# The first recurrence's triangular inverse in 32x32 blocks on four array tiles

## What is computed

```python
def step(S, inp):
    r_t, w_t, k_t, v_t, a_t, b_t = inp
    sa = jnp.einsum("bhvk,bhk->bhv", S, a_t)
    S = S * w_t[:, :, None, :] + sa[..., None] * b_t[:, :, None, :] + v_t[..., None] * k_t[:, :, None, :]
    y = jnp.einsum("bhvk,bhk->bhv", S, r_t)
    return S, y
```

## Time and profile before

| what | value |
|---|---|
| median of the timed runs | 2913.34 us |
| lowest and highest | 2909.52, 2915.71 us |
| span of the profiled execution, first to last instruction | 2905.3 us |
| mean granted TensorE clock in it | 0.995 |
| TensorE busy, of that span | 2814.7 us (97%) |
| VectorE, ScalarE, GpSimd busy | 2000.2, 1014.0, 1119.4 us |

### The profile page before, as it was taken

The page is one execution under the profiler, slowest core; times in us unless marked ns, Lnnn a source line. Parts: engine busy times, 40 slices in busy tenths (PEclk is TensorE's granted clock), DMA queues, the critical chain, the costliest instruction groups (busy, mean ns, idle before and its releaser), DMA issues. The chain is left out here.

```text
span 2905.3 us, 55296 instructions
## 1 busy us (share of the span) xinstructions
PE 2814.7 (97%) x21636; PEld 2455.6 (85%) x21636; DVE 2000.2 (69%) x3205; ACT 1014.0 (35%) x1492; POOL 1119.4 (39%) x873
## 2 busy tenths in 40 slices
PE   8999999999999999998999999999999999999998
PEld 6787888787888888877999999999978888888886
DVE  6898865568777777777466768784436676676655
ACT  3131644434333333345222333224323333332333
POOL 0001432317655566550222232231314655555552
PEclk9999999999999999999999999999999999999999
DMA  4111000322111111124111111123421112111112
GB/s 130 46 49 39 4 3 25 110 73 62 48 50 58 47 56 49 49 83 138 42 54 57 33 52 31 52 65 113 146 81 44 51 47 61 47 54 51 47 47 87
DMA packets 205344, 173.09 MB, mean 60 GB/s; under 512 B 10573, under 2 KB 182053, under 8 KB 204773
## 3 DMA queue, kind: packets, MB, share of 16 engines
q1 hardware_dynamic: 198245, 161.88, 18.2%
q10 hardware_dynamic: 6912, 8.52, 0.8%
HBM read 149.27 MB, written 21.10 MB: 59 GB/s over the span
## 5 line engine op out<-in xcount | busy, mean ns | idle before, releaser
L3103 DVE TENSOR_TENSOR tokens_x<-ffn_acc,tokens_x 128x512 f32<-128x512 f32 x450 | 302.2, 688 | 67.0 <-PE ffn_acc L2659 66.9
L3922 PE MATMUL mix_e<-blk_hi,mix_w_hi 128*128 128x348 f32 (+3 forms) x1056 | 343.4, 325 | 2.4 <-DVE blk_lo L3058 1.2
L3922 PE MATMUL mix_e<-blk_lo,mix_w_hi 128*128 128x348 f32 (+3 forms) x1056 | 339.1, 321 | 0.0
L3922 PE MATMUL mix_e<-blk_hi,mix_w_lo 128*128 128x348 f32 (+3 forms) x1056 | 338.0, 320 | 0.0
L2642 PE MATMUL ffn_out<-ffn_T,ffn_w12h 128*128 128x512 f32 x1008 | 313.0, 392 | 5.6 <-POOL ffn_w12l L2520 3.5
L2659 PE MATMUL ffn_acc<-blk_hi,ffn_hid_hi 128*128 128x512 f32 x900 | 309.7, 393 | 1.3 <-issue 1.3
L3489 POOL TENSOR_TENSOR mix_w_lo<-mix_raw,mix_w_hi 128x1024 fp32r<-128x1024 f32 x44 | 107.9, 2452 | 366.9 <-ACT mix_w_hi L3524 366.9
L2520 POOL TENSOR_TENSOR ffn_w03l<-ffn_r,ffn_w03h 128x512 fp32r<-128x512 f32 x126 | 193.1, 1533 | 122.5 <-ACT ffn_w03h L2871 118.9
L2642 PEld LDWEIGHTS ffn_out<-ffn_T,ffn_w12h 128*128 128x128 f32 x1008 | 188.5, 189 | 45.8 <-POOL ffn_w12l L2520 4.4
L2520 POOL TENSOR_TENSOR ffn_w12l<-ffn_r,ffn_w12h 128x512 fp32r<-128x512 f32 x114 | 167.7, 1480 | 106.9 <-ACT ffn_w12h L2871 104.9
L3922 PEld LDWEIGHTS mix_e<-blk_hi,mix_w_hi 128*128 128x128 f32 x1056 | 198.4, 188 | 6.2 <-issue 3.5
(11 more groups left out here) (538 smaller groups left out, 7028.6 us busy)
## 6 DMA issues: line engine op xcount, KB each, us to landing
ffn_r<-ffn_up SPq DMA_DIRECT2D x88, 256.0 KB, 3.0
mix_raw<-w_in SPq DMA_DIRECT2D x44, 512.0 KB, 3.9
ffn_r<-w_up SPq DMA_DIRECT2D x88, 256.0 KB, 3.0
ffn_room<-ffn_down SPq DMA_DIRECT2D x20, 512.0 KB, 4.0
ffn_room<-w_down SPq DMA_DIRECT2D x20, 512.0 KB, 4.1
proj_w_raw<-w_in_first SPq DMA_DIRECT2D x19, 512.0 KB, 3.8
branch_gates<-proj SPq DMA_DIRECT2D x16, 520.0 KB, 4.7
wout_raw<-w_out SPq DMA_DIRECT2D x16, 512.0 KB, 3.7
```

The source lines that it names most:

```text
L3103: return vec.tensor_tensor(dst, accs[t % len(accs)], dst, ALU.add)
L3922: last = nc.tensor.matmul(dst[:, 0:m], a[n % 2][:, kd, :], b[:, kd, c:c + m], start=kd == 0 and part_ == 0, stop=kd == KD - 1 and part_ == 2)
```

## The change

The inverses after level 4 are two 32x32 blocks on the diagonal of each 64x64 matrix, so levels 1 to 4 are done on these blocks alone. The tensors `xt`, `xx` and the masks' products become `[128, 16, 32]`: partitions 0 to 31 hold the first block of head 0, 32 to 63 the second, and so on (`quads`). Each of the four groups of 32 partitions has its own 32x32 tile of the array. The sixth level works on the corner that joins the two.

```diff
 def level_t(l, b, q):
-    pe.wait_ge(lm_ready, 12 * q + 2 * l + b + 1)
+    if l < LEVELS - 1:
+        pe.wait_ge(lm_ready, 10 * q + 2 * l + b + 1)
+    else:
+        await_taken(pe, "lba1", q)
...
     for i in range(8):
-        for hd in heads:
-            last = mm(lv[hd, b, i * C1:(i + 1) * C1], lm[l % 2][hd, 8 * b + i, :], xx[hd, 8 * b + i, :],
-                      start=True, stop=True, skip_group_check=True)
+        m = 8 * b + i
+        if l < LEVELS - 1:
+            for rows_ in quads:
+                last = mm(lv[rows_, b, i * HALF:(i + 1) * HALF], lm[l % 2][rows_, m, :], xx[rows_, m, :],
+                          start=True, stop=True, skip_group_check=True)
+        else:
+            for rows_, to in (quads[0:2], quads[2:4]):
+                last = mm(lv[to, b, i * HALF:(i + 1) * HALF], lba[rows_, 1, m, :], xx[rows_, m, :],
+                          start=True, stop=True, skip_group_check=True)
 def level_x(l, b, q):
...
-        first, second = (xt, tt) if l < LEVELS - 1 else (tt, xt)
-        for hd in heads:
-            last = mm(lv[hd, b, i * C1:(i + 1) * C1], first[hd, m, :], second[hd, m, :], start=True, stop=True,
-                      skip_group_check=True)
+        if l < LEVELS - 1:
+            for rows_ in quads:
+                last = mm(lv[rows_, b, i * HALF:(i + 1) * HALF], xt[rows_, m, :], tt[rows_, m, first_half],
+                          start=True, stop=True, skip_group_check=True)
+        else:
+            for hd, rows_ in ((heads[0], quads[1]), (heads[1], quads[3])):
+                last = mm(lv[hd, b, i * HALF:(i + 1) * HALF], tt[rows_, m, :], xt[rows_, m, :],
+                          start=True, stop=True, skip_group_check=True)
+def inner_scores(x, q):
+    out = start_piece(f"lba{x}", q)
+    for m in range(BLOCKS):
+        for n in range(2 if x else 4):
+            hd, to = heads[n if x else n // 2], quads[2 * n if x else n]
+            keys_ = first_half if x or n % 2 == 0 else last_half
+            last = mm(out[to, m * HALF:(m + 1) * HALF], source(0, m, q)[hd, keys_],
+                      ar[q % 2][hd, m, 0, last_half if x or n % 2 else first_half], start=True, stop=True,
+                      skip_group_check=True)
+    end_piece(last, f"lba{x}", q)
 def level_out(l, b, q):
-    activation(tt[:, blocks(b), :], by_chunk(lv[:, b, :]), ACT.Copy).then_inc(tt_ready, 1)
+    activation(tt[:, blocks(b), first_half], by_half(lv[:, b, 0:8 * HALF]), ACT.Copy).then_inc(tt_ready, 1)
 def last_level(b, q):
-    vec.tensor_tensor(eight("xtf", q, b), by_chunk(lv[:, b, :]), xt[:, blocks(b), :], ALU.add).then_inc(
-        xtf_ready, 1)
+    vec.tensor_copy(eight("xtf", q, b)[:, :, last_half], by_half(lv[:, b, 0:8 * HALF])).then_inc(xtf_ready, 1)
+def unit_columns():
+    pool.wait_ge(projected.psum_free, 22)
+    nc.gpsimd.tensor_copy(tt[:, :, last_half], eye.unsqueeze(1).broadcast_to((P, BLOCKS, HALF))).then_inc(
+        eye_ready, 1)
+def first_columns(q):
+    for b in range(2):
+        pool.wait_ge(xt_ready, 10 * q + 8 + b + 1)
+        if q:
+            pool.wait_ge(u_ready, 4 * q)
+        nc.gpsimd.tensor_scalar(eight("xtf", q, b)[:, :, first_half], xt[:, blocks(b), :], upper, None,
+                                ALU.mult).then_inc(first_rows_ready, 1)
```

More of the change, by code:

```diff
@@ L38 @@
 NC1 = T // C1
+HALF = C1 // 2
 PAIRS = H // 2
@@ L691, in at @@
             return Scope(nc, "rec1", at=offset)
-        rows, inner = [P, PAIRS * QTOK], [P, BLOCKS, C1]
+        rows, inner, narrow = [P, PAIRS * QTOK], [P, BLOCKS, C1], [P, BLOCKS, HALF]
         kept = at(KEPT1)
         masks = {}
-        for name in ("head_ones", "levels", "eye"):
+        for name in ("head_ones", "inner"):
             masks[name] = kept.sb(name, [P, CONST_AT[name][1]])
+        kept.at = KEPT1 + 4 * (P + 6 * C1 + C1)
+        eye, upper = masks["inner"][:, 5 * HALF:6 * HALF], masks["inner"][:, 6 * HALF:6 * HALF + 1]
         both = kept.sb("both", [P, 2, C1])
@@ L765, in recurrence1 @@
         heads = [slice(0, N), slice(N, P)]
+        first_half, last_half = (slice(0, HALF), slice(HALF, C1))
+        quads = [slice(HALF * n, HALF * n + HALF) for n in range(4)]
         def eight(name, q, b):
@@ L899, in gpsimd @@
         def gpsimd(pool):
-            mask_level, receptance_key, conv_sum = gpsimd_pieces(pool)
+            mask_level, unit_columns, first_columns, receptance_key, conv_sum = gpsimd_pieces(pool)
             pool.wait_ge(projected.product_ready, 22)
@@ L906, in gpsimd @@
             for i in range(QUARTERS):
-                for l in range(LEVELS):
+                for l in range(LEVELS - 1):
                     if i or l >= 3:
                         mask_level(l, i)
+                first_columns(i)
                 if i + 1 < QUARTERS:
@@ L972, in scores_out @@
             def scores_out(q):
[L973 to L978 removed]
+                for x in range(2):
+                    await_piece(act, f"lba{x}", q)
+                    if q and x == 0:
+                        act.wait_ge(lm_ready, 10 * q)
+                    if q and x:
+                        act.wait_ge(t_ready, 10 * q)
+                    activation(lba[:, x], by_half(bank(f"lba{x}", q)), ACT.Copy).then_inc(taken(f"lba{x}", q), 1)
             def level_out(l, b, q):
                 act.wait_ge(t_ready, 10 * q + 2 * (l - 1) + b + 1)
[L982 removed]
+                activation(tt[:, blocks(b), first_half], by_half(lv[:, b, 0:8 * HALF]), ACT.Copy).then_inc(tt_ready, 1)
             def chain_g(c, q):
@@ L1670, in result_spread, with removal_scores @@
                     spread("yx", h, q, y_inv)
-            def removal_scores(b, q):
+            def removal_scores(x, q):
                 pe.wait_ge(bk_ready, 2 * q + 1)
                 pe.wait_ge(ar_ready, 3 * q + 1)
-                scores(f"lba{b}", range(8 * b, 8 * b + 8), 0, q, slice(0, 1))
+                inner_scores(x, q)
             def conv_mean():
```

48 lines of the change are left out of this document (29 added, 19 removed).

## The result

The changed kernel takes 2979.12 us (median of 4 runs, 2972.47 to 2984.99) against 2912.88 for the kernel before beside it (4 runs, 2909.52 to 2915.71): a ratio of 1.0225, interval 1.0209 to 1.0241. It is 2.2% slower. The forecast was 2902 us.

The account below looks back on a forecast made before the run. TensorE's own throughput was taken to bound the kernel. Pairs -32.4, switches +15.5 and other engines +5.5 gave -11.4 us, from 2913.3 to about 2902 us; range 2891 to 2953, the forecast's own 2893 to 2907.

Parts of the forecast that it names:

- term 1: TensorE's load-and-matmul pairs in the inverse: 2816 become 5376, but 82.2 us falls to 49.8, a gain of 32.4 us.
- two tiles double the rate: Argument against rival A: two tiles give a pair each 29.2 ns where one tile has 58.4, so tiles overlap.
- Term 2, the switches: TensorE groups starting late after a change of weight shape: 103 switches at 0.15 us cost 15.5 us (12 to 31).
- Term 3, the other engines: Shorter VectorE, ScalarE and GpSimd steps, but lost cover makes TensorE wait: 5.5 us given back.
- Worth something only where TensorE waits for them: Claim that TensorE's throughput sets the time, so VectorE's and ScalarE's shorter instructions help only during TensorE's waits; no size given.
- rival C: Clock falls to 1.2 GHz, each costing about 1.7 us; ten more would cost 17 us, ending at 2919; 6%.
- Rival A: Four tiles don't overlap enough, or TensorE's feed limits pairs: 2956 us at 20 ns a pair, 2982 at 25; 27%.
- p: Rival A's ns per pair whatever the tile, from feed or array: 5120p + 7.5 us; it decides from 12.7.
- The PSUM rule: Skill's rule that row tiles can't share a PSUM bank at once; the four would take turns, giving the 25 ns case.
- Rival B: Half way, about no change: p near 10 or switches at 0.30 us, 2911 to 2918 us; 16%.
- What would show it: Signs in TensorE's timeline: 64 pairs in about 0.5 us, a level about 6.9 us, the stretch about 11 us shorter.
- the sum of waits for other engines: Sign of a wrong forecast: TensorE's waits for VectorE, ScalarE or GpSimd grow by more than 6 us in sum.

Follow-up runs that it names:

- the streams: Kernels computing nothing of the reference, only independent f32 matmul streams without waits; in the first, the first 255 pairs of 32x32 on four tiles start 8.4 ns apart.
- The quarter kernel: Changed kernel with only every fourth 32x32 matmul of levels 1 to 4, each with 128 moving columns: 2916.58 us, 1.0016 of the kernel before.
- the 64x64: Changed kernel with one 64x64 matmul a head, 32 moving columns, instead of two 32x32 ones in levels 1 to 4: 2935.17 us, ratio 1.0087.
- the wide one: Changed kernel with all matmuls of levels 1 to 4 kept, each over 64 moving columns instead of 32: 2978.15 us, 1.0235 of the kernel before.
- the first kernel of streams: Streams only, of 64x64 on two tiles, 32x32 on four and one, bursts, turns, bf16; 64x64 took 29.3 ns a pair, 32x32 on four tiles 29.3 with stops.
- the stream of 32x64: In the second streams-only kernel, 32x32 weights with 64 moving columns on four tiles instead of 32: 14 ns a pair inside a block, periods of 3.51 us.
- the stream on one tile: In the first streams-only kernel, 384 pairs on one tile instead of four: a pair each 31 to 32 ns at full clock, 53 to 55 at 1.2 GHz.

## Why the prediction was wrong

**The failed step is in term 1:** "I take 30 ns for a tile's period ... 7.5 ns a pair on four tiles". As a price of the array it was nearly right: 8.4 ns, and 0.68 us for 64 pairs and a switch. Its 30 ns for a tile's period was right too: one tile alone takes 31 to 32. As the price in the program it was wrong, because I priced pairs by what tiles can take, not by what reaches them. The count was right: 2560 pairs more by the code, (17730 - 12866)/2 = 2432 by the trace, and 128 of quarter 0's scores ahead of the stretch. What decided was blocks: 5120 instructions are 20 blocks more. The medians differ by 66.2 us, 3.3 a block, where term 1 had 32.4 us less. Of the profiled 70.2 us, 48.2 stand in stops for the feed and 12.2 in places without a stop at the 1.2 GHz level; the other 10 aren't split. The prediction had the doubt written down ("TensorE has to be fed two instructions a pair ... my forecast wants one each 3.75 ns over hundreds in a row"), with 12.5 ns as the fastest in sight, and gave it 27%. What hid the limit is that the kernel before lies just on it: the earlier trace rows show 32 pairs in 0.94 us, 14.7 ns an instruction, and I read that number only as a tile's 58.4 ns. Both readings fit that row; only a stream with more instructions tells them apart. For the same reason "two tiles double the rate" wasn't in the rows: none had one 64x64 tile by itself, and the 58.4 ns were the pair's 29.2 doubled.

**Term 2, the switches:** 0.15 us a switch was right (0.11 to 0.14 in the streams). Whether the 15.5 us stand in the sum isn't shown: the run with 36 switches fewer can't resolve its 5.4 us.

**Term 3, the other engines:** the 5.5 us given back didn't come. The waits for VectorE, ScalarE and GpSimd fell from 19.0 to 16.9 us, since a slower TensorE left them their cover. "Worth something only where TensorE waits for them" held for VectorE's and ScalarE's shorter instructions.

**Even fed, the forecast would have failed.** The quarter kernel has my price of a level (6.6 us) and the switches in full, and is 5 us slower than before, not 11 faster. 38 us more at 1.2 GHz stand there; at rival C's price, 1.7 us for each 3.4, that would be 19 us, about the 16 that are missing. For 6.3 us of it the trace shows the same pairs at the lower level; for the rest it is argued. There are also 4.6 us of stops in L1581, the scores' new form. What brings the clock down in this kernel, with 5.7 us of stops in all, stays open.

**Rival A** gave 2982 us for p = 25, and its condition "if feed or array gives a pair each p ns whatever the tile" came true by the feed. Its number is partly luck: the pairs' real pace under the feed is 29 ns, by which its sum would be near 3003 us with its 15.5 for switches. "The array doesn't overlap" is false. Its half of the rule from the Trainium skill (TensorE: Matmul & The Clock Gate, "Wait — 56ns, not 53.3ns?", starts never under about 25 ns apart) holds by tile at most: four tiles start a pair each 8.4 ns. The PSUM rule of the Trainium skill that the prediction weighed (TensorEngine Tiling (Array Packing), Gotcha 1: PSUM Pressure) would have made row tiles take turns in one bank; the earlier trace rows could not contradict that, as no row had one such tile alone; the streams do, with four tiles on one bank at 8.4 ns a pair and one tile alone at 31 to 32.

**Rival B** wanted p near 10 or 0.30 us a switch; the kernel is far outside its 2911 to 2918 us. **Rival C** was right that new falls come, and they cost at least 12.2 us, near its 17, beside the feed. They don't simply follow the stops: the 64x64 and the quarter kernel have 5.7 us of stops and 44.4 and 41.0 us at 1.2 GHz, the wide one 34.8 and 30.7. **What would show it**: "a 32x32 group takes over 0.8 us (A)" was too coarse a mark, and so was the sum of waits for other engines. Unbroken groups take 0.68, and cut ones far more; the row to watch was the wait for "issue".

## What to carry to other kernels

Count TensorE's instructions, not only its columns: an f32 matmul is four, and this program got 256 of them each 3.5 to 3.75 us. Before anything is cut into smaller tiles, work out instructions x 14.5 ns beside the array's time, and do it for stretches of a few hundred instructions, since only about 500 lie ready. A level gives 736 x 14.5 ns = 10.7 us, as measured; the whole stretch gives 17730 x 14.5 ns = 257 us and hides the loss, because its slow parts can't lend their time to the fast ones. If the two times are near each other, smaller tiles can only lose. In the profile, idle time before "issue" that cuts a group of equal matmuls in its middle is this limit, and the packets of the instruction queue count the blocks.

## What the runs showed of the hardware

- In bursts, four 32x32 tiles start a pair each 8.4 ns (255 pairs), one tile alone one each 31 to 32 ns. On four tiles TensorE then stood still after 478 and 510 instructions of a stream; a burst of 384 had no stop.
- A tile's period for an f32 pair went with the larger of weight columns and moving columns: about 34 ns for 32 and 32 (4 x 8.4), 56 for 32 and 64, 58 for 64 and 32 as for 64 and 64, 110 to 115 for 128 moving columns with either weights. With several tiles at work these are the pair's spacing times the number of tiles.
- While the feed binds, the 1.2 GHz level costs little: a block took 3.75 us in the stream at a clock of 0.50 and 3.51 in the one at full clock, and the wide kernel with 58 us less of it has the changed kernel's median. Where the feed doesn't bind it costs: 224 pairs took 13.92 us instead of 7.47.
- Stops and the lower clock don't go together one to one: the stream of 32x64 stopped for 1.5 us in each 3.5 and kept full clock from 112.50 to 130.05 us, while the clock fell in the stream on one tile, which had no stop (0.68 over 174.0 to 190.6 us).
- bf16 doesn't lift the limit: 128 pairs of 32x32 in bf16 came each 3.45 to 4.0 us in the first kernel of streams, one load and one matmul a pair, as in f32. Yet a bf16 matmul is one such pair where an f32 matmul is two.
